# A streaming encoder step on one core: the output projection by token tile, a split router, and a first expert selected without the table

## The chip, the cores and the metric

The kernel runs on one core of one Trainium2 chip. Its time is device time in microseconds. Three runs of the kernel before gave a median of 1534.97 us (1534.58 to 1539.33). Engines are called as in the profile: PE (matmuls), PEld (its weight loads), DVE (vector), ACT (scalar, with activation functions), POOL (GpSimd), SP (the engine that issues nearly all transfers). A "q" behind a name, as in SPq, is that engine's sequencer.

## What is computed

The reference is one inference step of a one-layer streaming encoder, in float32, for 256 tokens of a prompt and 64 tokens of a running stream, all 1024 wide:

```python
mix = jax.nn.sigmoid(ga) * y_att + jax.nn.sigmoid(gb) * y_conv
xp = layer_norm(DN_ALPHA * xp + mix @ w_out[l] + b_out[l], ln1_g[l], ln1_b[l])
ff = moe(xp.reshape(B * S, D_MODEL), w_router[l], b_router[l], w_gate[l], ...)
xp = layer_norm(DN_ALPHA * xp + ff, ln2_g[l], ln2_b[l])
```

`y_att` is chunked band attention, `y_conv` a depthwise convolution with its own norm; both come from one input projection. The stream's 64 tokens go the same way with caches. `moe` is a router over 32 experts: logits from `x @ w_router + b_router`, the 4 largest per token, a softmax over these 4, and for each chosen expert a clamped SwiGLU, `h = gt * sigmoid(1.702 * gt) * (up + 1)`, `h @ w_down + b_down`, summed with the softmax weights. Every expert has three matrices of 1024x1024, 4 MB each: 12.6 MB an expert, 403 MB for all.

## The kernel before

The 320 tokens are three tiles: 128, 128 and 64 rows (`TT`, numbered 0, 1, 2). SBUF holds six weight buffers of 4 MB, `WG`, `WU` and `WD`, each twice, for experts of even and of odd place. In the dense part the same memory holds the activations and a ring of two halves (`ring[0]`, `ring[1]`, 512 columns each) through which the dense weights pass; `WG[1]` is the ring's own memory, `WD[1]` holds `xtok` and `x1T`. The program of each engine is written out by hand, engine by engine, and semaphores set the order; nothing is planned by a tool. In a `wait_ge` the engine's sequencer stops, and all that follows it on that engine waits too.

Around the change the order is this. SP asks for the two halves of `w_out` when the attention's output product has used the ring's halves (line 275, `ao_mm` 4 and 8). PE multiplies half by half: for each half `s`, for each token tile, 8 matmuls of 512 columns into one PSUM bank (line 1132). DVE adds each result to `xtok` (L755), takes statistics (L758), and behind the second half normalises a tile (L761 to L775); ACT supplies the square root (L548). The result is `xs`, kept with channels regrouped. PE transposes tiles 0 and 1 (L1147), ACT copies them out chunk by chunk (L557), PE computes their logits (L1154), then the same for tile 2 with DVE's copy (L794). DVE then does the router for all three tiles at once (L799 to L823): bias, the 8 largest, their indices, one-hot terms, softmax, the mask `chosen`.

From the mask PE counts each token's rank within its expert (L1180), DVE makes `rank`, sorts the experts (a key comparison; places alternate large and small experts, experts 0 and 1 stand first) and writes three tables: `tbl` (the first block of each expert), `nblk`, `order` (L845 to L855, then `tables_done`). A block is up to 32 tokens of one expert. POOL compares ranks with slot numbers to make the selector `sel` (L428 to L437) and copies one-hot columns, `hot` (L441, L442). PE gathers the block's tokens with `sel` (L1214) and turns them (L951).

The loop runs over 16 pairs of experts, and inside over their blocks, 58 in all here. For each pair PE's sequencer loads three table entries into registers:

```python
starts = [pe.value_load(tbl[0:1, bass.ds(q * 2 + k, 1)], min_val=0, max_val=200) for k in range(3)]
```

A block is: gate product (L1231, 64 passes of 32-column weights in four column strips), the previous block's combine (L1254), up product (L1231), gather for the next block, transposes, down product (L1296). SP reloads each half of a weight buffer when the last block of its expert has used it (L235). ACT fills `yacc`, the sum's start, with the scaled `xs` ahead of the loop (L585, L590), and DVE adds each block's result (L867).

## Time and profile before

| what | value |
|---|---|
| median of three runs | 1534.97 us |
| the profiled execution's own time | 1536.92 us |
| its span | 1535.2 us |
| PE busy | 1413.4 us, 92% |
| DVE, ACT, POOL busy | 569.7, 283.5, 116.5 us |
| HBM read | 454.09 MB |
| mean granted clock of PE | 0.965 |

Busy time alone says little here: PE is busy for nine tenths of the span, and the transfers run near their rate for long stretches too, but not in the same stretches throughout. In the profile's 40 slices (38.4 us each) the transfers stand still at about 620 to 650 us, and from 960 to 1490 no slice leaves them below nine tenths. A granted clock of 1.0 is 2.4 GHz, 0.5 is 1.2 GHz; a window between the two had part of each.

### The profile page before, as it was taken

Reading aid. Unit: us, or ns where it says so; the run is one execution under the profiler, and the core shown is the slowest. Engines: PE = TensorE matmul, PEld = TensorE weight load, DVE = VectorE, ACT = ScalarE, POOL = GpSimd, SP = SyncE. Lnnn points to the kernel's source line nnn. Section 1 sums busy time; section 2 is a strip of 40 time slices with the busy share of each in tenths; the row PEclk is TensorE's granted clock in tenths of the full one; section 3 lists DMA queues with packets and bytes.
Section 4 is the critical chain, followed back from the end, with each engine's and each line's share of the span. In section 5 each row is a group of like instructions: output and inputs, shape, how many; then the busy total and the mean of one; then the engine's idle time right before and its main releaser. Section 6 shows DMA issues by size and latency. Waiting matters only on the chain.

```text
span 1535.2 us, 41624 instructions
## 1 busy us (share of the span) xinstructions
PE 1413.4 (92%) x17082; PEld 796.0 (52%) x17083; DVE 569.7 (37%) x1080; ACT 283.5 (18%) x600; POOL 116.5 (8%) x327
## 2 busy tenths in 40 slices
PE   7999999888996899999999999999998998879994
PEld 4777674466644445555545445454454454335542
DVE  1069962233216233332333333333232332213325
ACT  0111211233011312112112112111111111111112
POOL 3500000000000110000010001000100010000100
PEclk9999999899997899999999999999999999999997
DMA  7343332510676797079799797999999999999990
GB/s 230 112 149 123 110 109 75 199 56 1 250 307 263 322 426 305 0 331 427 294 429 423 319 427 301 403 426 425 426 429 424 426 427 426 425 428 428 423 412 34
DMA packets 62981, 458.63 MB, mean 299 GB/s; under 512 B 4325, under 2 KB 6997, under 8 KB 30158
## 3 DMA queue, kind: packets, MB, share of 16 engines
q1 hardware_dynamic: 62698, 457.98, 72.6%
q10 hardware_dynamic: 259, 0.33, 0.1%
q8 instruction: 15, 0.25, 0.1%
q14 instruction: 9, 0.07, 0.0%
HBM read 454.09 MB, written 4.73 MB: 299 GB/s over the span
## 4 chain that ended last, share of the span: by engine, by line
PE 79%; DMA 11%; DVE 4%; issue 2%; ACT 2%; SPq 2%; ACTq 0%; POOLq 0%; POOL 0%; DVEq 0%
PE PS L1231 23%; PE PS L978 14%; PE PS L1296 12%; DMA SB<-in_w_down_dram 10%; PE PS L1254 6%; PE PS L1214 5%; PE PS L951 4%; PE PS L1132 3%; PE PS L1020 3%; PE PS L1111 2%; SPq L235 2%; ACT SB L515 1%; PE PS L1237 1%; PE PS L1241 1%; DMA SB<-in_state_conv_dram 1%
## 5 line engine op out<-in xcount | busy, mean ns | idle before, releaser
L1231 PE MATMUL PS<-SB 128*32 128x256 f32 x7424 | 438.5, 389 | 53.1 <-issue 32.5
L1231 PEld LDWEIGHTS PS<-SB 128*32 128x32 f32 x7424 | 239.5, 112 | 234.7 <-issue 74.2
L867 DVE SCALAR_TENSOR_TENSOR SB<-PS,SB 128x1024 f32<-128x1024 f32 x177 | 194.9, 1101 | 82.1 <-PE PS L1254 82.1
L1296 PE MATMUL PS<-SB 128*32 128x256 f32 x3712 | 213.4, 381 | 4.5 <-DMA SB<-in_w_down_dram 4.5
L978 PE MATMUL PS<-SB 128*128 128x320 f32 x768 | 209.8, 437 | 0.0
L978 PEld LDWEIGHTS PS<-SB 128*128 128x128 f32 x768 | 147.3, 192 | 61.7 <-issue 1.9
L878 DVE TENSOR_SCALAR PS<-PS 128x256 f32<-128x256 f32 x58 | 25.1, 432 | 410.3 <-PE PS L1241 410.3
L1296 PEld LDWEIGHTS PS<-SB 128*32 128x32 f32 x3712 | 114.1, 110 | 85.5 <-issue 9.8
L1254 PE MATMUL PS<-SB 32*128 32x256 f32 (+1 forms) x1416 | 124.0, 419 | 4.0 <-DVE SB L867 3.4
L670 DVE SCALAR_TENSOR_TENSOR SB<-SB 128x350 f32<-128x350 f32 x240 | 118.6, 575 | 0.0
L951 PE MATMUL PS<-SB 128*128 128x128 f32 (+6 forms) x406 | 85.2, 313 | 26.4 <-DVE SB L729 14.2
L1214 PE MATMUL PS<-SB 128*32 128x256 f32 (+1 forms) x1416 | 97.9, 390 | 7.3 <-POOL SB L437 7.3
L598 ACT COPY SB<-PS 128x256 f32<-128x256 f32 x58 | 21.6, 372 | 393.3 <-PE PS L951 393.3
L951 PEld LDWEIGHTS PS<-SB 128*128 128x128 f32 (+6 forms) x406 | 49.4, 164 | 86.3 <-issue 38.7
L885 DVE TENSOR_SCALAR PS<-PS 128x256 f32<-128x256 f32 x58 | 25.1, 432 | 144.8 <-PE PS L1241 144.8
L596 ACT ACT_TABLE_LOAD x58 | 74.4, 1283 | 1.0
L441 POOL CAST SB<-SB 128x1 bf16 x58 | 10.8, 186 | 802.2 <-PE PS L1287 802.2
L1214 PEld LDWEIGHTS PS<-SB 128*32 128x32 f32 (+1 forms) x1416 | 34.0, 108 | 61.8 <-issue 51.8
L1254 PEld LDWEIGHTS PS<-SB 32*128 32x128 f32 (+1 forms) x1416 | 49.3, 166 | 27.0 <-DVE SB L867 4.2
L428 POOL TENSOR_TENSOR SB<-SB 128x96 f32<-128x96 f32 x58 | 20.4, 352 | 526.8 <-issue 523.8
L596 ACT ACTIVATE SB<-PS 128x256 f32<-128x256 f32 x58 | 22.2, 383 | 201.8 <-DVE PS L878 201.8
L604 ACT COPY SB<-PS 128x256 f32<-128x256 f32 x58 | 21.6, 372 | 193.9 <-PE PS L1296 193.9
(203 smaller groups left out, 974.4 us busy)
## 6 DMA issues: line engine op xcount, KB each, us to landing
SB<-in_w_gate_dram SPq DMA_DIRECT2D x64, 2048.0 KB, 25.2
SB<-in_w_up_dram SPq DMA_DIRECT2D x64, 2048.0 KB, 30.4
SB<-in_w_down_dram SPq DMA_DIRECT2D x64, 2048.0 KB, 32.5
SB<-in_w_in_dram SPq DMA_DIRECT2D x14, 2048.0 KB, 8.0
SB<-in_w_pw_dram SPq DMA_DIRECT2D x2, 2048.0 KB, 11.0
SB<-in_w_att_o_dram SPq DMA_DIRECT2D x2, 2048.0 KB, 7.9
SB<-in_w_out_dram SPq DMA_DIRECT2D x2, 2048.0 KB, 8.8
SB<-rev_bias SPq DMA_DIRECT2D x1, 2048.0 KB, 7.8
```

Of the source, the lines that this page charges most:

```text
L235: eng.dma_start(buf[:, 4 * h:4 * h + 4, :], src[:, step * h:step * h + step, :]).then_inc(sem(f"{name}_{h}"), 16)
L596: act.activation(tin, PS[:, 0, 0:256], ACT.Sigmoid, scale=SW_ALPHA).then_inc(sem("sig"), 1)
L670: dve.scalar_tensor_tensor(yc[:, c, :], uext[:, c, bass.ds(k, CONVN)], dwT[:, c, bass.ds(k, 1)], yc[:, c, :], ALU.mult, ALU.add).then_inc( ...
L867: dve.scalar_tensor_tensor(y, ps, gcol[:, tt:tt + 1], y, ALU.mult, ALU.add).then_inc(sem("yadd"), 1)
L951: return pe.transpose(out, in_, ident[0:k, 0:k])
L978: ins = pe.matmul(PS[:, t, 0:T], ring[s][:, c, P * t:P * t + P], xT[:, c, :], start=(c == 0), stop=(c == KC - 1))
L1020: ins = pe.matmul(PS[0:r, bank, :], xT[:, c, t0:t0 + r], ring[s][:, c, :], start=(c == 0), stop=(c == KC - 1))
L1132: ins = pe.matmul(PS[0:r, 3 * s + tt, :], mixT[:, c, t0:t0 + r], ring[s][:, c, :], start=(c == 0), stop=(c == KC - 1))
L1214: ins = pe.matmul(PS[32 * q:32 * q + 32, 2, 0:256], sel[r, tt, :], x_part(tt, q // 2)[:, k], start=(tt == 0), stop=(tt == 2))
L1231: ins = pe.matmul(PS[32 * q:32 * q + 32, bank, 0:256], xg[:, c % 2, c // 2, :], buf[:, c, 256 * q:256 * q + 256], start=(c == 0), stop=False)
L1254: ins = pe.matmul(out, scat[r, TT[tt][0]:sum(TT[tt])], ysb[r, :], start=True, stop=True)
L1296: ins = pe.matmul(PS[32 * n:32 * n + 32, 2, 256:512], hT[:, ck % 2, ck // 2, :], WD[par][:, ck, 256 * n:256 * n + 256], start=(ck == 0), s ...
```

## The change

- **Output projection.** For each token tile, both halves: PE waits for both halves of `w_out` first, then multiplies tile 0, tile 1, transposes tile 0, multiplies tile 2. Tile 2's halves go to partitions 0 to 63 and 64 to 127 of one bank. ACT copies the second half of tile 2's `xtok` to the upper partitions beforehand.
- **Norm and router.** DVE normalises tile by tile. ACT copies each transposed tile in one operation. Tiles 0 and 1 go through the router together, tile 2 alone; the sort's constants and those of the tables are set between the two. The order of experts is sent to PE's queue ahead of the ranks' transposes.
- **First selector.** POOL makes `sel0` for expert 0 right from `rank`, and PE gathers with it before the tables are there. POOL's loop is as before, with its own wait on `sel_ready`; what it makes for block 0 is not used.
- **Tables.** A fourth table `tbl3` packs three block numbers into one integer; PE loads one entry a pair and unpacks it in registers. The wait on `hot_ready` moves from the block's start to the middle of the gate product.
- **The sum `yacc`.** Its start is computed on DVE instead of ACT.

```diff
-            sp.wait_ge(sem("out_mm"), 6)
+            sp.wait_ge(sem("out_mm"), 3)
             load_halves(sp, WG[1], wg_v[1], "wg1")
...
-            sp.wait_ge(sem("logit_mm"), 1)
+            sp.wait_ge(sem("logit_mm"), 2)
             load_halves(sp, WD[1], wd_v[1], "wd1")
...
-            for name in ("gsig", "h_ready", "y_sb", "hT_ready", "bc_mm", "gath_mm"):
+            for name in ("gsig", "h_ready", "y_sb", "hT_ready", "bc_mm", "gath_mm", "sel_ready"):
...
+            pool.wait_ge(sem("rank_ready"), 1)
+            link(pool.tensor_tensor(sel0, rank[:, :, 0:1].broadcast_to([P, 3, SLOTS]),
+                                    iota.rearrange("p (a s) -> p a s", a=1).broadcast_to([P, 3, SLOTS]), ALU.subtract))
+            pool.tensor_scalar(sel0, sel0, 0.0, None, ALU.is_equal).then_inc(sem("sel0_ready"), 1)
...
                     pool.wait_ge(sem("gath_mm"), i + 1)
+                    pool.wait_ge(sem("sel_ready"), i + 1)
...
+            def turned_x1(tt):
+
+                act.wait_ge(sem("x1T_mm"), tt + 1)
+                act.copy(x1T[:, :, P * tt:P * tt + P], PS[:, 2 * tt:2 * tt + 2, :].rearrange("p b (c n) -> p (b c) n", c=4))\
+                   .then_inc(sem("x1T_a"), 1)
+
+            act.wait_ge(sem("xr_ready"), 3)
+            act.copy(xtok[64:128, 2, 512:D], xtok[0:64, 2, 512:D]).then_inc(sem("xr2_ready"), 1)
             std1(0)
+            act.wait_ge(sem("v_out"), 32)
+            turned_x1(0)
             std1(1)
+            turned_x1(1)
             std1(2)
 
-            act.wait_ge(sem("v_out"), 32)
-            for c in range(KC):
...
+                act.wait_ge(sem("top_ready"), 1 + tt // 2)
...
-            act.wait_ge(sem("tables_done"), 1)
...
-            for tt in range(3):
...
-                        act.activation(dst, src, ACT.Copy, scale=ALPHA).then_inc(sem("y_init"), 1)
...
+            act.wait_ge(sem("tables_done"), 1)
...
-            for s in range(2):
-                for tt, (_, r) in enumerate(TT):
-                    dve.wait_ge(sem("out_mm"), 3 * s + tt + 1)
...
+            def norm1(tt):
+
+                r = TT[tt][1]
+                v = xtok[0:r, tt, :]
+                dve.wait_ge(sem("out_mm"), tt + 1)
+                if tt < 2:
+                    w = v.rearrange("p (s n) -> p s n", s=2)
+                    dve.tensor_tensor(w, w, PS[:, 2 * tt:2 * tt + 2, :], ALU.add).then_inc(sem("x1_pre"), 1)
+                else:
+                    for s in range(2):
+                        c, k = slice(512 * s, 512 * s + 512), slice(64 * s, 64 * s + 64)
+                        ins = dve.tensor_tensor(xtok[0:r, 2, c], xtok[k, 2, c], PS[k, 4, :], ALU.add)
+                    ins.then_inc(sem("x1_pre"), 1)
+                dve.wait_ge(sem("x1_pre"), tt + 1)
+                for s in range(2):
+                    ins = dve.bn_stats(stats[0:r, tt, 6 * s:6 * s + 6], xtok[0:r, tt, 512 * s:512 * s + 512])
+                link(ins)
...
+            def largest(tiles, bank):
+
+                n = tiles.stop - tiles.start
+                link(dve.tensor_tensor(lg[:, tiles, :], PS[:, bank, 0:n * E].rearrange("p (t e) -> p t e", t=n),
...
+                dve.tensor_scalar(ntop[:, tiles], top8[:, tiles, 0], -1.0, None, ALU.mult).then_inc(sem("top_ready"), 1)
+
+            def shares(tiles):
+
+                n = tiles.stop - tiles.start
+                for tt in range(tiles.start, tiles.stop):
+                    ins = dve.max_index(idx8[:, tt, :], top8[:, tt, :], lg[:, tt, :])
...
+            dve.wait_ge(sem("logit_mm"), 1)
+            largest(slice(0, 2), 5)
+            dve.wait_ge(sem("v_out"), 32)
+            dve.wait_ge(sem("x1T_mm"), 3)
+            for half in range(2):
+                ins = dve.tensor_copy(x1T[:, 4 * half:4 * half + 4, NP_:T], PS[:, 4 + 3 * half, 0:256].rearrange("p (c n) -> p c n", c=4))
+            ins.then_inc(sem("x1T_d"), 1)
+            shares(slice(0, 2))
+
             link(dve.tensor_copy(tie, iota[0:E, 0:E]))
...
+            link(dve.memset(one_r, 1.0))
+            link(dve.memset(starts, 0.0))
+
+            dve.wait_ge(sem("logit_mm"), 2)
+            largest(slice(2, 3), 6)
+            shares(slice(2, 3))
...
             dve.wait_ge(sem("order_mm"), 1)
-            link(dve.tensor_copy(order, PS[0:1, 2, E:2 * E]))
-            link(dve.tensor_copy(cnt, PS[0:1, 2, 0:E]))
...
             link(dve.tensor_scalar(nb, nb, 1.0, None, ALU.max))
-            link(dve.memset(one_r, 1.0))
-            link(dve.tensor_tensor_scan(cum, one_r, nb, 0.0, ALU.mult, ALU.add))
-            link(dve.memset(tbl[:, 0:1], 0))
-            link(dve.tensor_copy(nblk, nb))
-            dve.tensor_copy(tbl[:, 1:E + 1], cum).then_inc(sem("tables_done"), 1)
+            link(dve.tensor_tensor_scan(starts[:, 1:E + 1], one_r, nb, 0.0, ALU.mult, ALU.add))
+            dve.tensor_copy(nblk, nb)
+            dve.tensor_copy(tbl, starts)
+            link(dve.scalar_tensor_tensor(three, starts[:, 1:E:2], 256.0, starts[:, 0:E:2], ALU.mult, ALU.add))
+            link(dve.scalar_tensor_tensor(three, starts[:, 2:E + 2:2], 65536.0, three, ALU.mult, ALU.add))
+            dve.tensor_copy(tbl3, three).then_inc(sem("tables_done"), 1)
+            dve.wait_ge(sem("tables_done"), 1)
+
+
+            for tt in range(2):
...
-            dve.wait_ge(sem("y_init"), 8)
...
-            for s in range(2):
-                pe.wait_ge(sem(f"ring{s}"), 16 * 10)
-                for tt, (t0, r) in enumerate(TT):
-                    if s == 1 and tt == 1:
-                        pe.wait_ge(sem("ktok_ready"), 6)
-                    for c in range(KC):
-                        ins = pe.matmul(PS[0:r, 3 * s + tt, :], mixT[:, c, t0:t0 + r], ring[s][:, c, :],
-                                        start=(c == 0), stop=(c == KC - 1))
-                    ins.then_inc(sem("out_mm"), 1)
-
...
+            def project(tt):
+
+                t0, r = TT[tt]
                 for c in range(KC):
-                    for tt in tiles:
-                        t0, r = TT[tt]
-                        src = x1_chunk(tt, c)
-                        o = 64 * (c // 4) if tt == 2 else 0
-                        ins = pe.transpose(PS[:, c, t0:t0 + r], src, ident[o:o + r, o:o + r])
-                    ins.then_inc(sem("x1T_mm"), 1)
+                    for s in range(2):
+                        if tt < 2:
+                            out = PS[:, 2 * tt + s, :]
+                        else:
+                            out = PS[64 * s:64 * s + 64, 4, :]
+                        ins = pe.matmul(out, mixT[:, c, t0:t0 + r], ring[s][:, c, :], start=(c == 0), stop=(c == KC - 1))
+                ins.then_inc(sem("out_mm"), 1)
...
+            def turn_x1(tt):
+
+                r = TT[tt][1]
+                pe.wait_ge(sem("x1_ready"), tt + 1)
...
-            pe.wait_ge(sem("x1_pre"), 6)
-            pe.wait_ge(sem("x1_ready"), 2)
-            transposed([0, 1])
-            pe.wait_ge(sem("x1T_a"), KC)
+            for s in range(2):
+                pe.wait_ge(sem(f"ring{s}"), 16 * 10)
+            project(0)
+            project(1)
+            turn_x1(0)
+            pe.wait_ge(sem("ktok_ready"), 6)
+            project(2)
             pe.wait_ge(sem("wr_in"), 32)
-            for tt in range(2):
-                logits(tt)
-            pe.wait_ge(sem("x1_ready"), 3)
-            transposed([2])
+            pe.wait_ge(sem("x1T_a"), 1)
+            logits(0)
+            turn_x1(1)
+            pe.wait_ge(sem("x1T_a"), 2)
+            logits(1).then_inc(sem("logit_mm"), 1)
+            turn_x1(2)
             pe.wait_ge(sem("x1T_d"), 1)
             logits(2).then_inc(sem("logit_mm"), 1)
...
+            for tt in range(2):
+                ranked(PS[:, 7, E * tt:E * tt + E], tt)
+            pe.wait_ge(sem("chosen_ready"), 2)
+            ranked(PS[:, 7, 2 * E:3 * E], 2)
...
+            pe.wait_ge(sem("at_place_ready"), 1)
+            for k in range(2):
+                ins = pe.matmul(PS[0:1, 6, E * k:E * k + E], cols[:, 1 + k:2 + k], at_place, start=True, stop=True)
+            ins.then_inc(sem("order_mm"), 1)
+
             pe.wait_ge(sem("rank_ready"), 1)
             for tt, (t0, r) in enumerate(TT):
                 ins = tr(PS[0:E, 5, t0:t0 + r], rank[0:r, tt, :])
             ins.then_inc(sem("rankT_mm"), 1)
...
-            def gather(need, free):
-
...
+            def gather(sel):
...
                         pe.wait_ge(sem(f"{loaded}_{c // 4}"), count)
+                    if c == 4 and hot_count is not None:
+                        pe.wait_ge(sem("hot_ready"), hot_count)
                     for q in range(Q):
...
+            pe.wait_ge(sem("sel0_ready"), 1)
+            gather(sel0)
+            turn_x(1)
...
-            gather(1, None)
-            turn_x(1)
             with pe.Fori(0, E // 2) as q:
-                starts = [pe.value_load(tbl[0:1, bass.ds(q * 2 + k, 1)], min_val=0, max_val=200) for k in range(3)]
+                three = pe.value_load(tbl3[0:1, bass.ds(q, 1)], min_val=0, max_val=200 * 65793)
+                starts = [three & 255, (three >> 8) & 255, three >> 16]
                 for par in range(2):
                     with pe.Fori(starts[par], starts[par + 1]) as i:
-                        pe.wait_ge(sem("hot_ready"), i * 2 + 2)
...
+                        gate_or_up(0, WG[par], f"wg{par}", q * 16 + 16, 0, "gate_half", "gate_done", i * 2 + 2)
...
-                        gather(i + 2, i + 1)
+                        pe.wait_ge(sem("sel_ready"), i + 3)
+                        pe.wait_ge(sem("tin_x"), i + 1)
+                        gather(sel)
```

## Rows read from the trace of the kernel before

**Rows 1.** Waits in the expert loop, 509 to 1513: total, times, longest.
```profile
PE PS L1231 <- issue: 32.5, 16, 2.6
```

**Rows 2.** Source view of L1264, 540 to 550: count, min/median/max ns, first and last start.
```profile
L1264 PEldq FUSED_REGOPS  x5: 51/151/156, 543.1 to 544.7; - x5
...
L1264 PEldq TENSOR_LOAD <-SB x3: 298/300/307, 542.8 to 544.4; - x3
```

**Rows 3.** Windows: length, busy time of five engines, clock, DMA share, GB/s.
```profile
946.00:962.00 16.00, 16.00 (x270) 8.46 (x266) 5.69 (x10) 3.06 (x6) 1.46 (x5) 1.00 0.22 78
...
962.00:1490.00 528.00, 484.99 (x7706) 251.05 (x7706) 168.18 (x296) 89.03 (x175) 42.07 (x145) 0.98 1.01 426
```

**Rows 4.** Source view of L235 around 543.7: one issue, its landing.
```profile
L235 SPq DMA_DIRECT2D SB<-in_w_down_dram x1: 384/384/384, 543.7 to 543.7; - x1
...
DMA to landing us min/median/max: 32.0/32.0/32.0
```

**Rows 5.** Source view of L235 around 790.3: one issue, its landing.
```profile
L235 SPq DMA_DIRECT2D SB<-in_w_down_dram x1: 383/383/383, 790.3 to 790.3; - x1
...
DMA to landing us min/median/max: 31.2/31.2/31.2
```

**Rows 6.** Timeline of PE at three down products: start, duration, what, idle before.
```profile
574.07 2.80 PE L1296 MATMUL PS<-SB 128*32 128x256 f32 x48
...
820.63 2.58 PE L1296 MATMUL PS<-SB 128*32 128x256 f32 x44
...
1376.26 1.93 PE L1296 MATMUL PS<-SB 128*32 128x256 f32 x32 [0.33 <-DMA SB<-in_w_down_dram]
```

**Rows 7.** Source view of L275, 425 to 445: the second half of w_out.
```profile
L275 SPq DMA_DIRECT2D SB<-in_w_out_dram x1: 379/379/379, 429.5 to 429.5; - x1
...
DMA to landing us min/median/max: 10.0/10.0/10.0
```

**Rows 8.** Timeline from the output projection to the first gate product.
```profile
431.94 41.85 PE L1132 MATMUL PS<-SB 128*128 128x512 f32 x96
...
473.82 0.68 DVE L755 TENSOR_TENSOR SB<-SB,PS 64x512 f32<-64x512 f32 x1 [0.66 <-PE PS L1132]
...
480.33 0.17 DVE L781 COPY SB<-SB 32x32 f32<-32x32 f32 x1
...
487.24 0.26 DVE L799 TENSOR_TENSOR SB<-PS,SB 128x96 f32<-128x96 f32 x1 [2.10 <-PE PS L1154]
...
491.12 0.21 DVE L823 TENSOR_SCALAR SB<-SB 128x96 bf16<-128x96 f32 x1
...
493.72 0.82 PE L951 MATMUL PS<-SB 128*32 128x128 f32 x3
...
494.92 0.18 DVE L845 CAST SB<-PS 1x32 int32<-1x32 f32 x1
...
497.29 0.17 DVE L855 CAST SB<-SB 1x32 int32<-1x32 f32 x1
...
502.20 2.94 PE L1214 MATMUL PS<-SB 128*32 128x256 f32 x24 [7.31 <-POOL SB L437]
...
505.69 0.69 PE L951 MATMUL PS<-SB 128*128 128x128 f32 x2 [0.55 <-ACT SB L570]
...
508.97 5.97 PE L1231 MATMUL PS<-SB 128*32 128x256 f32 x64 [2.59 <-issue]
```

**Rows 9.** Timeline of PE behind a wait in attention.
```profile
296.65 2.54 PE L951 MATMUL PS<-SB 128*128 128x128 f32 x10 [4.26 <-DVE SB L729]
```

**Rows 10.** Windows behind that wait and behind the first gate product.
```profile
300.00:310.00 10.00, 10.00 (x49) 7.82 (x49) 3.12 (x7) 3.28 (x15) 0.00 (x0) 0.72 0.00 1
...
512.00:516.00 4.00, 4.00 (x60) 1.82 (x54) 0.00 (x0) 2.55 (x3) 0.00 (x0) 0.79 0.58 180
```

**Rows 11.** Source view of L235, 473 to 474: first half of expert 1's w_gate.
```profile
DMA to landing us min/median/max: 7.3/7.3/7.3
```

**Rows 12.** Source view of L235, 487.2 to 487.6: expert 1's w_down, both halves.
```profile
DMA to landing us min/median/max: 14.8/17.1/19.3
```

More of the change, by code:

```diff
@@ L201, in encoder_step @@
         nb = view(R0 + 784, E, rows=1)
-        cum = view(R0 + 816, E, rows=1)
-        one_r = view(R0 + 848, E, rows=1)
-        above_n = view(R0 + 880, E, MAXB, rows=1)
+        sel0 = view(R0 + 2208, 3, SLOTS)
+        one_r = view(R0 + 816, E, rows=1)
+        starts = view(R0 + 848, E + 2, rows=1)
+        three = view(R0 + 1432, E // 2, rows=1)
+        above_n = view(R0 + 882, E, MAXB, rows=1)
         tri = view16(R0 + 2048, BF16, P)
@@ L445, in _ @@
             pool.wait_ge(sem("gath_mm"), total + 1)
+            pool.wait_ge(sem("sel_ready"), total + 1)
             pool.tensor_tensor(sel, sel, sel, ALU.subtract).then_inc(sem("sel_ready"), 1)
@@ L578, in _ @@
             turned()
-            for tt in range(3):
-                for half in range(2):
-                    if tt < 2:
-                        dst = yacc[:, D * tt:D * tt + D].rearrange("p (q c) -> p q c", c=KC)[:, :, 4 * half:4 * half + 4]
-                        src = x_part(tt, half).rearrange("p (c q) -> p q c", c=4)
-                        act.activation(dst, src, ACT.Copy, scale=ALPHA).then_inc(sem("y_init"), 1)
-            for half in range(2):
-                dst = yacc[64 * half:64 * half + 64, 2 * D:2 * D + 512].rearrange("p (q c) -> p q c", c=KC)
-                for k in range(2):
-                    src = x_part(2, k).rearrange("p (c q) -> p q c", c=4)[:, 64 * half:64 * half + 64, :]
-                    act.activation(dst[:, :, 4 * k:4 * k + 4], src, ACT.Copy, scale=ALPHA).then_inc(sem("y_init"), 1)
+            act.wait_ge(sem("tables_done"), 1)
             total = act.value_load(tbl[0:1, E:E + 1], min_val=1, max_val=200)
@@ new lines, in _ @@
+            for tt in range(3):
+                norm1(tt)
+            dve.wait_ge(sem("x1_ready"), 3)
+            dve.wait_ge(sem("wr_in"), 32)
+            def largest(tiles, bank):
+                n = tiles.stop - tiles.start
+                link(dve.tensor_tensor(lg[:, tiles, :], PS[:, bank, 0:n * E].rearrange("p (t e) -> p t e", t=n),
+                                       br_bc.rearrange("p (a e) -> p a e", a=1).broadcast_to([P, n, E]), ALU.add))
+                for tt in range(tiles.start, tiles.stop):
+                    ins = dve.max(top8[:, tt, :], lg[:, tt, :])
+                link(ins)
+                dve.tensor_scalar(ntop[:, tiles], top8[:, tiles, 0], -1.0, None, ALU.mult).then_inc(sem("top_ready"), 1)
@@ L781, in _ @@
+            dve.wait_ge(sem("logit_mm"), 1)
+            largest(slice(0, 2), 5)
+            dve.wait_ge(sem("v_out"), 32)
+            dve.wait_ge(sem("x1T_mm"), 3)
+            for half in range(2):
+                ins = dve.tensor_copy(x1T[:, 4 * half:4 * half + 4, NP_:T], PS[:, 4 + 3 * half, 0:256].rearrange("p (c n) -> p c n", c=4))
+            ins.then_inc(sem("x1T_d"), 1)
+            shares(slice(0, 2))
             link(dve.tensor_copy(tie, iota[0:E, 0:E]))
@@ L1181, in ranked @@
                 return ins
-            for tt in range(3):
-                ranked(PS[:, 1, E * tt:E * tt + E], tt)
+            for tt in range(2):
+                ranked(PS[:, 7, E * tt:E * tt + E], tt)
+            pe.wait_ge(sem("chosen_ready"), 2)
+            ranked(PS[:, 7, 2 * E:3 * E], 2)
             for s, (_, r) in enumerate(TT):
-                ins = pe.matmul(PS[:, 1, 3 * E:4 * E], ones16[0:r], chosen[0:r, s, :], start=(s == 0), stop=(s == 2))
+                ins = pe.matmul(PS[:, 7, 3 * E:4 * E], ones16[0:r], chosen[0:r, s, :], start=(s == 0), stop=(s == 2))
             ins.then_inc(sem("rank_mm"), 1)
@@ L1192, in _ @@
             ins.then_inc(sem("gT_mm"), 1)
+            pe.wait_ge(sem("at_place_ready"), 1)
+            for k in range(2):
+                ins = pe.matmul(PS[0:1, 6, E * k:E * k + E], cols[:, 1 + k:2 + k], at_place, start=True, stop=True)
+            ins.then_inc(sem("order_mm"), 1)
             pe.wait_ge(sem("rank_ready"), 1)
@@ L1197, in _ @@
             ins.then_inc(sem("rankT_mm"), 1)
-            pe.wait_ge(sem("at_place_ready"), 1)
-            for k in range(2):
-                ins = pe.matmul(PS[0:1, 2, E * k:E * k + E], cols[:, 1 + k:2 + k], at_place, start=True, stop=True)
-            ins.then_inc(sem("order_mm"), 1)
-            def gather(need, free):
-                pe.wait_ge(sem("sel_ready"), need)
-                if free is not None:
-                    pe.wait_ge(sem("tin_x"), free)
+            def gather(sel):
                 for tt in range(3):
@@ L1223, in turn_x, with gate_or_up @@
                 ins.then_inc(sem("trx_mm"), 1)
-            def gate_or_up(bank, buf, loaded, count, which, half, done):
+            def gate_or_up(bank, buf, loaded, count, which, half, done, hot_count=None):
                 for c in range(KC):
```

119 lines of the change are left out of this document (56 added, 63 removed).

## Prediction, made before the changed kernel was run

> **What bounds the kernel now.** I read the page's slices first, then the waits, the loop's windows and last a timeline of the stage that is rewritten. The run has three stretches. Up to 509 us it is the dense part, where matmuls follow each other with waits between. From 509 to 1512 it is the loop over 58 expert blocks. Two things alternate there. PE works without a pause in most blocks: its idle time of its own is 16 gaps of about 2 us, one per pair of experts [rows 1]. The weight stream is the other: from 962 to 1490 it moves 426 GB/s at a DMA share of 1.01, while just before, from 946 to 962, it stood at 0.22 because PE had not yet freed a buffer [rows 3]. So up to 960 PE sets when the stream restarts. From there the stream sets the pace, until PE's last wait on a weight ends at 1376.26 [rows 6]; after it PE alone sets the end. There are four such halts of the stream (600 to 659, 750 to 760, 851 to 858, 950 to 960; the row is of the last). A shift of the first block therefore runs through to the end, but a gain made inside the loop survives only where no landing stands behind it.
>
> Two landings decide that. The last half of w_down of expert 3 is issued at 543.7 and lands 32.0 later, at 575.7 [rows 4]; PE begins that product at 574.07 and needs the half 1.8 us in (64 passes at 58 ns, from 48 in 2.80), at 575.9 [rows 6]. There is no room (0.2). For expert 9 it is 790.3 + 31.2 = 821.5 against 820.63 + 1.8 = 822.4, room 0.9 [rows 5, 6]. Experts 6 and 12, the other two at the end of such a run of transfers, have 2.9 and 4.4 by the same reckoning.
>
> **The output projection.** Before: 48 matmuls (96 passes) in 41.85 us from 431.94, 6.98 per tile and half [rows 8]. It could start because only the first half of w_out was asked for. The second half is issued at 429.5 and takes 10.0, so it lands at 439.5 [rows 7]. The new order asks for both halves ahead of the first matmul, and all of PE is queued behind that wait: PE starts at 439.5, 7.6 later than now. Tiles 0 and 1 cost 4 x 6.98 = 27.9. The 64-row tile's two halves run in two column strips at once: one pass of 512 columns takes 0.436 (41.85 / 96), which is 0.218 for 256 columns, and the loop's four strips take 0.058 a pass, 3.8 times less; so strips overlap nearly fully and I take 7.0 instead of 14.0. Ends: 7.0, and 14.0 if they don't overlap. Tile 0's transposes come between: 8 of them, 1.0 (an estimate from three small ones in 0.82 at the lower clock).
>
> The wait also costs clock. After an idle of 4.26 the granted clock fell to 1.2 GHz and was there for 56% of the next ten us, although PE ran [rows 9, 10]. At the first gate product it came back 4.7 us after the start (0.79 over 512 to 516) [rows 8, 10]. The wait here is longer, so I take the fall as sure, 4.7 us at half rate, loss 2.3; ends 0 and 4.5 (nine us low, as in attention). The projection then ends at T = 439.5 + 27.9 + 1.0 + 7.0 + 2.3 = 477.7, against 473.8 before. So this part alone makes things 3.9 later.
>
> **What T decides.** Expert 1's w_gate goes into the ring's place and is issued at T. Its first half lands 7.3 after issue, at 481.1 [rows 11], and the last half of its w_down at 487.6 + 19.3 = 506.9 [rows 12]: 33.1 from issue to the sixth half. The issue of w_down moves with the router from 487.2 to 490.6, while the stream has work to 499: nothing. Before, the stream then stood still until 512.8. If the first reload is issued early enough, it now follows without a pause, 12 more halves of 2.097 MB at 426 GB/s = 4.92 each to expert 3's last one: T + 33.1 + 59.0 = 569.8 against 575.7. The stream gains 5.9, or 483.6 - T in general.
>
> **Norm, router, tables.** Tile 2's norm is last: before, 6.5 us from the projection's end to 480.33 [rows 8]. It now has a second addition and a second statistics pass behind that end (0.7 each, by the 0.68 row), 7.9 in all: 485.6. Tile 1's norm ends at 477.4 and is not in the way, but ACT is: the square root of tile 2 is queued behind the copy of tile 1's transposes, and these stand on PE behind tile 2's projection and tile 0's logits (2.4 and 1.0, copy 1.1, so 482.2), where DVE would want it at 480.8. That wait costs 1.4: x1 is ready at 487.0 (480.3 before). Transposes 0.7, copies 0.8, logits 1.9 end at 490.6. DVE meanwhile does the router of two tiles, and now the constants too, which stood under a wait before: 0.9 + 0.8 + 2.5 + 1.1 to 492.3. Then tile 2's router alone: three tiles took 487.24 to 491.33 = 4.1, most of it fixed cost, one tile 2.6 as an estimate: 494.9, which is 3.5 later than before.
>
> Behind it a lot goes. The tables come 6.1 behind the mask (497.46), now 0.2 less: 500.8. The order is on DVE 2.5 ahead of them, so PE is through with it at 498.2 and turns the ranks in 0.8: 499.0. The selector for expert 0 no longer waits for the tables and POOL's three loads; its two POOL operations are done by then. Gather 2.94, copy 0.5: the transposes start at 502.4. From their start to the gate it was 3.28 with three table loads; with one it is 2.1: gate at g = 504.5 against 508.97, 4.5 earlier. The reload is issued 3.9 behind g and lands 7.3 after: 515.7, where the stream allows 515.7 (481.1 + 3.9 + 25.8 + 4.9). So the stream's 5.9 just holds; each microsecond that g is later takes one away.
>
> **The yacc initialisation** moves from ACT to DVE, which idled until the first clamp: eight operations, at most 6.2 us from 500.8, three loads 2.4: 509.4; the first clamp is due at 511. Nothing; if DVE is late by 2, PE waits for less than that. **The hot wait** moves from the gate's start to its middle: POOL writes it for later blocks long before; nothing, at most 0.1 a block either way. **POOL's own wait** on the selector: nothing.
>
> **One table load instead of three.** Loads start 0.8 apart (542.8 to 544.4) [rows 2]. Two fewer is 1.6; unpacking adds four register operations, which take 0.05 to 0.15 each: 0.4. That leaves 1.2 a pair. Ends: -0.2 (the unpacking costs what the loads did) and 1.7. Where it counts: at the second pair it is lost to expert 3's landing (no room). Pairs 3 and 4 keep 2.4 (room 2.9), pair 5 keeps 0.9 of 1.2 (expert 9), pairs 6 and 7 keep 2.4 (room 4.4): 5.7 by 960. Then seven pairs are lost to the stream. The last two (gaps before 1396 and 1462) keep 2.4. Sum 8.1.
>
> **The sum.** 5.9 + 8.1 = 14.0; nothing changes behind 1512. The profiled execution took 1536.92 for a span of 1535.2; the median shown is 1534.97, so 1536.92 - 14.0 = 1522.9 would be that execution's twin, and from the median it is 1521.0, which I take.
>
> **A page of the skill weighed.** The Trainium skill, "TensorE: Matmul & The Clock Gate", section "Measured speedup vs the span model", has three column strips at 2.38 times, not 3. By that rate two strips give 1.6, tile 2 costs 8.8 and the time is 1522.8. The trace has 3.8 of 4 and I go by it; the page's rate has 5 of the forecast's 59 chances in 100.
>
> **Rivals.**
> (A) The strips run one after another: T = 484.7, the stream gains -1.1, total 7.0: 1528.0. Against it stands the 0.058. 8%.
> (B) The pair savings don't arrive, 5.9 alone remains: 1529.1. For it: assertion and unpacking also take register time [rows 2]; against it: the loads' spacing. 12%.
> (C) The clock doesn't fall at the wait: T = 475.4, the stream gains 8.2 and g moves along, total 16.3: 1518.7. 8%.
> (D) The chain through ACT and DVE is 4.5 longer than summed: the first gate comes no earlier than now and 8.1 remains: 1526.9. For it: every step of it is linked to the one before; against it: most steps are rows of the old chain. 8%.
> (E) Slower. The clock falls at the wait and does not come back during the projection: 69.8 instead of 34.9, T = 511.3 with the transposes, the stream loses 27.7, total 19.6 later: 1554.6. It decides from 33 us at the low rate, where T passes 491.7. For it: nine low us behind the attention wait [rows 9, 10]; against it: these are the densest matmuls of the kernel. 5%.
> The Trainium skill, same page, section "Loop structure matters more than you think", speaks for (E): matmuls that stand behind a wait for a transfer run cold. The trace agrees that they start so.
>
> **Numbers.** Forecast 1521.0, 59%, its own range 1517 to 1525 (clock 0 to 4.5, load 1.0 to 1.7, g). The range 1515 to 1529.5 takes in A to D. 0.3%, 4.6 us, is about what a measurement of this kernel can tell from no change. Faster: the forecast and A to D but for the thin end of B and D, 0.91; within 0.3%: 0.04; slower: E, 0.05.
>
> **What would show it.** Right: PE idle for 7.6 before the projection with a clock below 1 behind it; 32 passes of 128x64 weights in 7.0; the first gate near 504.5; gaps between pairs at 0.8; a stream with no halt between 480 and 600; PE waiting over a microsecond for expert 3's w_down. Wrong: a first gate after 506, gaps near 2.0, or the projection ending past 480.

## The result, and the profile after

The changed kernel took 1516.34 us (median of 4, 1514.17 to 1518.34), the kernel before beside it 1535.43 (1534.58 to 1539.33): a ratio of 0.987, 95% interval 0.985 to 0.989. That is 19.1 us less, where 14.0 was forecast. The span of the profiled execution went from 1535.2 to 1512.5, 22.7 less. A repeat of the changed kernel, below called the repeat, gave 1516.42 (4 runs) with a profiled span of 1515.6. One run of a version below, the one that keeps PE busy while it waits, was a slow one (1617.63, at a granted clock of 0.871) and is left out of that version's median.

The rewritten stage, timeline of PE and DVE in the kernel after:

```profile
436.93 29.19 PE L1180 MATMUL PS<-SB 128*128 128x512 f32 x64 [6.85 <-DMA SB<-in_w_out_dram]
466.93 7.09 PE L1180 MATMUL PS<-SB 128*64 128x512 f32 x32
473.94 1.97 PE L1198 MATMUL PS<-SB 128*128 128x32 f32 x16
478.09 0.15 DVE L775 RECIPROCAL SB<-SB 64x1 f32<-64x1 f32 x1 [1.10 <-ACT SB L557]
490.58 0.18 DVE L829 TENSOR_SCALAR SB<-SB 128x32 bf16<-128x32 f32 x1
494.88 2.94 PE L1262 MATMUL PS<-SB 128*32 128x256 f32 x24
496.78 0.17 DVE L886 CAST SB<-SB 1x16 int32<-1x16 f32 x1
500.25 5.35 PE L1281 MATMUL PS<-SB 128*32 128x256 f32 x64 [1.50 <-issue]
```

PE waits 6.85 for w_out's second half, the two strips of tile 2 take 7.09, ACT holds DVE for 1.10, the gather starts ahead of the last table copy, and the first gate product comes at 500.25. Against [rows 8] everything from there on is sooner.

Waits of PE in the loop (total, times, longest), then windows (columns as in [rows 3]) and SP's issues:

```profile
PE PS L1281 <- DMA SB<-in_w_up_dram: 15.0, 9, 2.2
PE PS L1349 <- DMA SB<-in_w_down_dram: 9.0, 8, 1.9
PE PS L1281 <- DMA SB<-in_w_gate_dram: 8.9, 5, 3.0
PE PS L1281 <- issue: 8.2, 15, 1.5
```

```profile
430.00:440.00 10.00, 3.15 (x5) 1.52 (x5) 0.00 (x0) 2.83 (x4) 0.00 (x0) 0.66 1.02 382
...
946.00:962.00 16.00, 16.00 (x270) 8.45 (x266) 5.69 (x11) 3.06 (x6) 1.46 (x5) 1.00 1.01 433
```

```profile
410.27 17.61 SPq L278 DMA_DIRECT2D SB<-in_w_out_dram  x2
474.05 0.81 SPq L238 DMA_DIRECT2D SB<-in_w_gate_dram  x2
503.05 3.51 SPq L238 DMA_DIRECT2D SB<-in_w_gate_dram  x2
```

In the wait and behind it the clock is low: 0.66 in the mean from 430 to 440. The 32.5 us that PE lost between pairs [rows 1] are 8.2, and a window in which the stream stood nearly still [rows 3] is now full of it, at 433 GB/s. Three more timeline rows of PE: a gap between pairs, and the waits for the last half of w_down of expert 3 and of expert 27, which is the last weight that PE waits for (1376.26 in [rows 6]):

```profile
534.63 3.66 PE L1281 MATMUL PS<-SB 128*32 128x256 f32 x64 [0.48 <-issue]
566.42 1.93 PE L1349 MATMUL PS<-SB 128*32 128x256 f32 x32 [1.32 <-DMA SB<-in_w_down_dram]
1358.21 1.93 PE L1349 MATMUL PS<-SB 128*32 128x256 f32 x32 [1.85 <-DMA SB<-in_w_down_dram]
```

These points cut the run in four. w_out is asked for at 412.28 in the profile of before:

| stretch | before | after | repeat | gain | forecast |
|---|---|---|---|---|---|
| start to the issue of w_out (code unchanged) | 412.3 | 410.3 | 411.2 | 2.0, 1.1 | 0 |
| to expert 3's last half | 163.4 | 156.1 | 158.3 | 7.3, 5.1 | 5.9 |
| to the last weight that is waited for | 800.6 | 791.8 | 791.8 | 8.8 | 5.7 |
| to the end | 158.9 | 154.3 | 154.3 | 4.6 | 2.4 |

The first line is no gain: over the profiles shown here, of fourteen executions, the unchanged dense part reaches that issue between 407.6 and 414.2. Without it the change is worth 20.7 and 18.5 in the two traces, 19.1 in the medians. The split between the other lines is good to about 2 us only: a second trace of the kernel before (below) has 161.6, 798.8 and 160.6 in them, where the first has 163.4, 800.6 and 158.9.

### The profile page after: what moved, and what is told of

Its sections match the earlier page's. It is cut to its first block, busy times and chain, and to the rows that moved or that the text cites. A ratio compares the mean times of both kernels' runs of the same rounds, so it can differ in the third digit from the quotient of the medians.

```text
span 1512.5 us, 41579 instructions
## 1 busy us (share of the span) xinstructions
PE 1405.4 (93%) x17082; PEld 790.8 (52%) x17083; DVE 575.4 (38%) x1100; ACT 277.7 (18%) x587; POOL 117.3 (8%) x329
## 4 chain that ended last, share of the span: by engine, by line
PE 72%; DMA 18%; DVE 4%; SPq 2%; ACT 2%; issue 1%; ACTq 0%; DVEq 0%
PE PS L1281 20%; DMA SB<-in_w_down_dram 17%; PE PS L1022 14%; PE PS L1349 11%; PE PS L1304 5%; PE PS L1262 5%; PE PS L995 3%; PE PS L1064 3%; PE PS L1155 2%; PE PS L1180 2%; SPq L238 2%; ACT SB L524 1%; PE PS L1287 1%; PE PS L1291 1%; DMA SB<-in_state_conv_dram 1%
## 5 line engine op out<-in xcount | busy, mean ns | idle before, releaser
L449 POOL CAST SB<-SB 128x1 bf16 x58 | 10.8, 186 | 778.7 <-PE PS L1340 778.7
L472 ACT ACTIVATE SB<-PS,SB 128x320 f32 x40 | 21.1, 528 | 130.5 <-PE PS L1022 130.4
```

## Experiments

The theory after the result, called the stream theory, in its last form: up to expert 27 the end is set by when weight halves land, and that hangs on two issues alone, expert 1's w_gate (behind the projection) and the first reload (in the first gate product). Behind expert 27 it is PE's work. The rivals are that each microsecond of PE's own work counts (work theory), and, for each part, that it did nothing. In the expectations it is an earlier form, in which the second issue has some room. All times are medians of 3 to 8 runs; the kernel before gave 1535.6, 1536.4 and 1535.9 in the three groups of runs.

**Three table loads instead of one.**

```diff
-three = pe.value_load(tbl3[0:1, bass.ds(q, 1)], ...)
-starts = [three & 255, (three >> 8) & 255, three >> 16]
+starts = [pe.value_load(tbl[0:1, bass.ds(q * 2 + k, 1)], ...) for k in range(3)]
```

> PE again loads three table entries a pair instead of one packed entry; all else as changed. Stream theory (a gain in the loop counts only where no landing of weights stands behind it): gaps of 2.0 instead of 0.48, 1.5 each, kept in the pairs 3 to 7 up to the room of the landings and in the last two; 8 to 10 us, and up to 13.4 if the granted clock falls again at some of the 2 us gaps: 1525 to 1530. Rival 1 (every gap counts): 15 x 1.5 = 23, 1539. Rival 2 (the loop is bound by transfers, gaps are worth nothing): 1516 to 1518.

Measured: 1528.35, ratio 0.995 (0.993 to 0.996), 11.9 more than the changed kernel, within the stream theory's 1525 to 1530 and far from both rivals. PE in its trace:

```profile
505.39 5.12 PE L1281 MATMUL PS<-SB 128*32 128x256 f32 x64 [3.01 <-issue]
672.00 3.66 PE L1281 MATMUL PS<-SB 128*32 128x256 f32 x64 [1.88 <-issue]
1370.31 1.93 PE L1348 MATMUL PS<-SB 128*32 128x256 f32 x32 [1.87 <-DMA SB<-in_w_down_dram]
```

A gap is 1.88 in place of 0.48, so the packed table saves 1.40 a pair, not 1.2. From expert 3's half (572.18) to 1370.31 it is 798.1 against 791.8 and from there to the end 157.0 against 154.3: the load is worth 6.3 and 2.7 there. The first reload, which is now the later of the two issues by 1.8 (last table), makes 10.8 of the 11.9.

**The packed table in the kernel before, alone.**

```diff
+dve.scalar_tensor_tensor(three, starts[:, 1:E:2], 256.0, starts[:, 0:E:2], ...)
+dve.scalar_tensor_tensor(three, starts[:, 2:E + 2:2], 65536.0, three, ...)
+dve.tensor_copy(tbl3, three).then_inc(sem("tables_done"), 1)
...
-starts = [pe.value_load(...) for k in range(3)]
+three = pe.value_load(tbl3[0:1, bass.ds(q, 1)], ...)
+starts = [three & 255, (three >> 8) & 255, three >> 16]
```

> The kernel before with the packed table alone: one table load in place of three at each pair, everything else of it as before. Stream theory: the first gate comes 1.4 earlier, and as the stream stands still then, expert 3's weights land 1.4 earlier; pairs 3 to 7 keep what the landings of experts 6, 9 and 12 leave room for (2.9, 0.8 and 2.9, with 1.7 more if the clock's fall at the gap before 874 goes too); after the last landing two gaps of 1.45 each, and 1.7 if the fall before 1462 goes. Sum 11.0 without the clock's falls, 14.4 with them: 1521.2 to 1524.6, and gaps of 0.5 us in place of 2.0. Work theory (all 16 gaps count): 23 less, 1512. The prediction's own price, 1.2 a pair and 8.1 in the loop: 1527.5. It also tells whether the falls of the clock at three of the gaps go with the gaps' length or with another part of the change.

Measured: 1521.37, ratio 0.991 (0.989 to 0.992). This one edit alone gives 15.0, where the whole change gives 19.1. Its gaps are 0.56 to 0.63, and no gap in its trace has a fallen clock behind it.

**The hot wait in the middle, in the kernel before, alone; and back at the start, in the changed kernel.**

```diff
 def gate_or_up(...):
     if c % 4 == 0: pe.wait_ge(sem(f"{loaded}_{c // 4}"), count)
+    if c == 4 and hot_count is not None: pe.wait_ge(sem("hot_ready"), hot_count)
 ...
-pe.wait_ge(sem("hot_ready"), i * 2 + 2)
```

> The kernel before with the hot wait in the middle of the gate's product, as in the changed kernel, and nothing else. The gaps between pairs should be 1.88 in place of 1.98 to 2.03. If the clock's falls at three of the gaps (5.35 in place of 3.66 for the product behind) hang on this tenth of a microsecond, they go, as in the changed kernel with three loads, and the time is 0.3 plus up to 3.4 less: 1532 to 1533. If they are a matter of chance or of place, they stay in part and the time is 1535 to 1536.

Measured: 1530.89, ratio 0.996 (0.995 to 0.998): 5.0 less for a tenth of a microsecond a gap, more than the 1532 to 1533 that were expected if the falls hang on it. The kernel before was traced once more:

> The kernel before once more, for a second trace of it. If the three falls of the clock at the gaps belong to the kernel, the products behind the gaps at about 874, 1058 and 1462 take 5.35 again; if they are chance, they stand elsewhere or there are more or fewer. Time as before: 1534 to 1539.

Measured: 1536.27. Gate products behind a gap in the first trace of before (one), in the second (four), then in that with the wait moved:

```profile
874.28 5.35 PE L1231 MATMUL PS<-SB 128*32 128x256 f32 x64 [2.00 <-issue]
```

```profile
872.59 3.66 PE L1231 MATMUL PS<-SB 128*32 128x256 f32 x64 [1.98 <-issue]
988.97 5.35 PE L1231 MATMUL PS<-SB 128*32 128x256 f32 x64 [1.99 <-issue]
1392.54 5.35 PE L1231 MATMUL PS<-SB 128*32 128x256 f32 x64 [2.01 <-issue]
1460.41 5.35 PE L1231 MATMUL PS<-SB 128*32 128x256 f32 x64 [1.98 <-issue]
```

```profile
872.84 3.66 PE L1233 MATMUL PS<-SB 128*32 128x256 f32 x64 [1.88 <-issue]
1458.77 3.66 PE L1233 MATMUL PS<-SB 128*32 128x256 f32 x64 [1.87 <-issue]
```

Each trace lists 14 such products between pairs. In the first of before 3 of 14 took 5.35 in place of 3.66 (at 874, 1058, 1462), in the second 4 (989, 1231, 1392, 1460); in the second, the 20 us from 1460 have a mean clock of 0.91, those from 860 have 1.00. With gaps of 1.87 to 1.93, here and with three loads above, none of 28 did, nor did any with the packed table (3.66 to 3.81). A fifteenth gap stands before half a product, 32 passes, and is not in these counts; behind it they took 1.93, but 2.41 in the second trace of before. So the clock's falls are chance in place, were seen, of the gaps between pairs, behind those of 1.97 to 2.03 alone, and cost 1.7 each where PE's work counts. The stretch behind expert 27 shows it in each trace: 157.0 without a fall, 158.9 with one, 160.6 with two. All this is for gaps in else dense work: among close waits for weights the clock is low around shorter ones too (in the kernel after 0.50 from 1338 to 1342, behind waits of 2.95 and 1.88), which costs nothing where the stream sets the pace.

The traces with and without each of the two edits, from expert 3's last half to the end:

| | hot wait at the start | hot wait in the middle |
|---|---|---|
| three loads | 959.5, 959.4 (before, twice) | 955.2, 955.1 (hot wait moved; three loads) |
| one packed load | 946.6, 946.2 (before with the packed table; the run that follows) | 946.1, 946.1 (changed, repeat) |

With three loads the hot wait is worth 4.3 here, with one load 0.1 to 0.5: either edit takes the falls away, and there is nothing left for the other to take. Only the sum is steady: against the two traces of before the moved wait gives 2.4 and 0.6 up to expert 27, and 1.9 and 3.6 behind it.

The other way round, in the changed kernel:

> The changed kernel with the hot wait back at the start of each block. For the first block POOL writes it 1.3 us behind the gate's start (504.18 against 502.87), so that gate comes 1.3 later; that lies within the room of the first reload. The gaps between pairs get 0.10 to 0.12 longer (0.48 to 0.58), and two of them count at the end. Stream theory: 0.2 to 0.5 more, 1516.6 to 1516.9. Work theory: 1.3 and 16 times 0.11, 3.1 more, 1519.5.

Measured: 1517.19 (ratio 0.988, 0.986 to 0.990), 0.8 more than the changed kernel and not to be told from it. Its trace shows the first gate waiting 3.30 for POOL's copy, the first reload at 503.72 and expert 3's half at 566.69; by the last table its first reload is the later issue by 1.9, so "within the room" was wrong.

**The strips one behind the other.**

```diff
 order = [(c, s) for c in range(KC) for s in range(2)]
+if tt == 2: order = [(c, s) for s in range(2) for c in range(KC)]
```

> Tile 2's two column strips are multiplied one after the other (8 matmuls of one strip, then 8 of the other) instead of in turn. Stream theory: the projection ends 7 us later (14 instead of 7.1) and the end 7 us later: 1523. Rival 1 (the strips overlap nothing anyway, or the time is hidden): 1516. Rival 2 (the first gate binds, and its chain absorbs part): 1518 to 1521.

Measured: 1521.28, ratio 0.990 (0.989 to 0.992), 4.9 more. Tile 2 in its trace:

```profile
472.35 12.29 PE L1182 MATMUL PS<-SB 128*64 128x512 f32 x32
484.57 0.63 PE L1200 MATMUL PS<-SB 128*128 128x32 f32 x4
```

12.29 against 7.09: what the order by turns saves is 5.2, not 7. Even strip by strip the 32 passes take less than the 14.0 of no overlap, apparently because the last passes of the one strip run beside the first of the other (the 2 us from 477 hold 10 passes, those before them 6). So the expected 1523 had the wrong price; at the right one the 4.9 is one for one with the projection's end. The second rival, that the first gate binds, was put at 1518 to 1521 and is not excluded by the time; in this trace the two issues stand 0.3 apart (last table). Side by side, the two strips' 32 passes (7.09) cost what 16 cost on full columns (6.98 in the forecast's rows).

**Tile 0 by halves**, so that PE starts before the second half of w_out lands.

```diff
+if tt == 0: order = [(c, s) for s in range(2) for c in range(KC)]
+if tt == 0 and c == 0: pe.wait_ge(sem(f"ring{s}"), 16 * 10)
...
-for s in range(2): pe.wait_ge(sem(f"ring{s}"), 16 * 10)
```

> Tile 0 is multiplied half by half again, so that PE waits for the second half of w_out only after 6.9 us of work; tiles 1 and 2 as changed. Stream theory: PE's idle of 6.85 before the projection and the 1.3 of low clock behind it go, the projection ends 8 us earlier and so does everything up to the end: about 1508. Rival (the projection's end is not what the stream waits for, a later link binds): less than 3 us, 1513 to 1516.

Measured: 1508.33, ratio 0.982 (0.981 to 0.984), 8.1 less than the changed kernel.

```profile
431.03 7.03 PE L1184 MATMUL PS<-SB 128*128 128x512 f32 x16
438.72 20.87 PE L1184 MATMUL PS<-SB 128*128 128x512 f32 x48 [0.66 <-DMA SB<-in_w_out_dram]
467.41 1.97 PE L1202 MATMUL PS<-SB 128*128 128x32 f32 x16
```

**PE kept busy in that wait**, without starting sooner.

```diff
+pe.wait_ge(sem("ktok_ready"), 6)
+for n in range(8): pe.matmul(PS[:, 7, :], mixT[:, n, 0:P], ring[0][:, n, :], ...)
+pe.wait_ge(sem("ring1"), 16 * 10)
```

> The changed kernel with eight extra matmuls of 128x512 on w_out's first half (16 passes, 7.0 us, into a bank that nothing reads) while PE waits for the second half. If the idle time is what lets the clock fall, it stays high: the first 64 passes of the projection take 27.9 in place of 29.2 to 29.7, and the time is 1.3 to 1.8 less, 1514.6 to 1515.1. If the fall comes from something else (the smaller products ahead of it), 1516.4. If the extra matmuls outlast the transfer, up to 1 us is given back and it is 1516 too, but the trace then shows passes at full clock.

```profile
428.37 7.10 PE L1205 MATMUL PS<-SB 128*128 128x512 f32 x16 [0.99 <-ACT SB L552]
435.31 27.67 PE L1180 MATMUL PS<-SB 128*128 128x512 f32 x64
```

The mechanism is shown: 27.67 for the 64 passes, against 29.19 in the kernel after and 29.65 in the repeat. The time, 1512.16 (3 runs; ratio 0.985, 0.983 to 0.987), is 4.3 less where 1.3 to 1.8 were due. In this trace w_out was asked for at 407.56, the earliest of all. From there to the end it takes 1102.0, where the changed kernel takes 1102.2 and the repeat 1104.4. So 0.2 to 2.4 are gained behind that issue, as due, and the rest is the start, in code that was not changed. Why it was early was not settled.

**Expert 1's w_gate asked for later.** Nothing else is touched.

```diff
 sp.wait_ge(sem("out_mm"), 3)
+sp.wait_ge(sem("logit_mm"), 1)
 load_halves(sp, WG[1], wg_v[1], "wg1")
```

> The changed kernel, with one wait more on SP alone: expert 1's w_gate is asked for when the logits of tiles 0 and 1 are through (484.1 in the trace of the changed kernel's repeat) in place of the projection's end (476.6). PE, DVE and ACT do what they did, and expert 1's last half still lands some 20 us before its use. Stream theory: every later landing moves by the 7.5, up to the stream's last one at 1361, and the time with it: 1523.9. Work theory (a transfer with 20 us of room costs nothing): 1516.4. Prediction's view, 1 for 1 as long as no halt stands behind: 1523.9 too, so this run tells only between the first two.

Measured: 1523.94, ratio 0.992 (0.991 to 0.993). PE's own part up to the gather is as in the repeat, and the last half of expert 1's w_down (issued 489.4, landing 27.9 later) is there 17 us before PE begins that product at 534.2. Still 7.5 us are lost, as the stream theory expected; the work theory had 1516.4:

```profile
483.84 0.82 SPq L238 DMA_DIRECT2D SB<-in_w_gate_dram  x2
506.72 3.59 SPq L238 DMA_DIRECT2D SB<-in_w_gate_dram  x2
```

```profile
476.69 1.97 PE L1199 MATMUL PS<-SB 128*128 128x32 f32 x16
576.22 1.93 PE L1350 MATMUL PS<-SB 128*32 128x256 f32 x32 [0.28 <-DMA SB<-in_w_down_dram]
1368.06 1.93 PE L1350 MATMUL PS<-SB 128*32 128x256 f32 x32 [0.28 <-DMA SB<-in_w_down_dram]
```

**The selector behind the tables again.**

```diff
 pool.wait_ge(sem("rank_ready"), 1)
+pool.wait_ge(sem("tables_done"), 1)
 link(pool.tensor_tensor(sel0, ...
```

> The changed kernel, but POOL builds the first expert's selector only after the wait for the tables, as before. In the trace of the changed kernel POOL would so begin 3.1 us later and the first gate product come 3.1 us later (506.0 in place of 502.9). Stream theory (what counts is when the weight halves land): the first reload, issued at 505.0, would be issued at 508.1 and land 7.3 to 10 later, at 515.4 or after; it landed at 515.3 in any case. So nothing is lost on the stream, and PE has 3.3 us of waits for weights up to expert 3's w_down that take the delay in: 1516.4 to 1518, the upper end if the clock falls in the longer wait. Work theory (every microsecond of the first gate counts): 1519.5. Prediction's statement that there is no slack and each microsecond of a later first gate costs one: 1519.5 as well.

Measured: 1520.52, ratio 0.989 (0.987 to 0.991), 4.1 more. The stream theory as it then stood expected 1516.4 to 1518 and missed; my room of 3.3 was wrong. The work theory's 1519.5, and the prediction's "each microsecond that g is later takes one away", were nearer. The second issue came into the theory after this run: the first reload comes 3.9 later behind the projection than in the repeat, and it is the later issue by 2.8 (table below). The gather begins 4.0 later behind the projection, not 3.1:

```profile
500.84 2.52 DVE L894 TENSOR_SCALAR SB<-SB 128x512 f32<-128x512 f32 x4
500.98 0.75 POOL L422 TENSOR_TENSOR SB<-SB 128x96 f32<-128x96 f32 x1 [441.29 <-DVE SB L887]
501.81 1.07 POOL L424 TENSOR_SCALAR SB<-SB 128x96 f32<-128x96 f32 x1
502.94 2.94 PE L1263 MATMUL PS<-SB 128*32 128x256 f32 x24 [4.13 <-POOL SB L424]
510.30 2.47 SPq L238 DMA_DIRECT2D SB<-in_w_gate_dram  x2
```

POOL's two operations take 0.75 and 1.07 beside the wide ones (128x512) of DVE's yacc initialisation, and in the repeat, with DVE at small work, 0.35 and 0.47:

```profile
494.89 0.35 POOL L421 TENSOR_TENSOR SB<-SB 128x96 f32<-128x96 f32 x1 [435.61 <-DVE SB L858]
495.33 0.47 POOL L423 TENSOR_SCALAR SB<-SB 128x96 f32<-128x96 f32 x1
```

The Trainium skill, "GPSIMD Engine Reference", section "1. Specifications", says that POOL shares its way into SBUF with the vector engine and contends with some of its forms. The slowing above fits that, but no run shows whether these operations are of those forms. Beside the narrower ones (64x256) that follow in the changed kernel, POOL's L436 takes 0.35 as ever.

**The chain to the first gate shortened**, on top of tile 0 by halves: the best version that these results point to.

```diff
 std1(1)
-turned_x1(1)
 std1(2)
+turned_x1(1)
```

(And the constants of the sort move behind `shares(slice(2, 3))` on DVE.)

> The split wait (projection of tile 0 by halves, 1508.3) with two steps taken out of the chain to the first gate: ACT takes tile 2's square root before it copies tile 1's transposes (DVE waited 1.1 for it), and the constants of the order stand behind the router of tile 2 in DVE's queue, where it waits for a bit of PE less (0.85). The first gate comes 1.1 to 2.0 earlier. Stream theory: the landings up to expert 12 hang on the projection's end alone and on the last ones of the ring, which don't move, so nothing is gained: 1508.0 to 1508.6. Work theory: 1506.4 to 1507.2.

Measured: 1507.25, ratio 0.982 (0.981 to 0.984), the same ratio as tile 0 by halves alone. Its first gate comes 24.4 behind the projection's end, where it was 26.2, and this bought nothing that can be measured. The run doesn't tell between the theories either: 1508.0 to 1508.6 and 1506.4 to 1507.2 were expected, and the interval is 2 us to either side. Both versions beat the changed kernel and the one before.

**One rule for all of them.** From the traces: when expert 1's w_gate is asked for (a), when the first reload is (b), and when expert 3's last half is there, by PE's wait or, in the first three lines, by issue and landing. The last columns test it: the later of a + 92.4 and b + 62.9.

| kernel | a | b | expert 3's half | a + 92.4 | b + 62.9 |
|---|---|---|---|---|---|
| before | 473.8 | 512.8 | 575.7 | 566.2 | **575.7** |
| before, second trace | 473.7 | 510.9 | 573.8 | 566.1 | **573.8** |
| before, hot wait moved | 472.6 | 512.0 | 574.7 | 565.0 | **574.9** |
| before, packed table | 472.5 | 508.3 | 571.3 | 564.9 | **571.2** |
| changed, three loads | 477.7 | 509.0 | 572.2 | 570.1 | **571.9** |
| changed | 474.1 | 503.1 | 566.4 | **566.5** | 566.0 |
| changed, repeat | 476.6 | 505.0 | 569.5 | **569.0** | 567.9 |
| PE kept busy | 470.9 | 499.1 | 563.5 | **563.3** | 562.0 |
| tile 0 by halves | 467.5 | 497.4 | 560.2 | 559.9 | **560.3** |
| and the shorter chain | 466.2 | 493.5 | 558.7 | **558.6** | 556.4 |
| strips apart | 484.7 | 513.9 | 577.1 | **577.1** | 576.8 |
| w_gate asked for later | 483.8 | 506.7 | 576.2 | **576.2** | 569.6 |
| hot wait at the start | 472.3 | 503.7 | 566.7 | 564.7 | **566.6** |
| selector behind tables | 478.0 | 510.3 | 573.2 | 570.4 | **573.2** |

It holds within 0.5 us in fourteen traces. The two constants were chosen on these same traces, and no run was forecast with them, so this is a fit and not a test; the forecast's own figure in place of 92.4 was 92.1. In the kernel before the reload was the later by 9.5; the change took that away, and now the two stand within 0.5 to 1.1 of each other.

## Why the prediction held, step by step

- **What bounds the kernel.** Right: the stream from T, then PE behind expert 27. T is not alone, though: the first reload is nearly as late. The asked-for-later w_gate cost 7.5 as computed.
- **The projection.** T was to come 65.4 behind the issue of w_out (477.7 less 412.3). The traces with the projection as changed give 63.4 to 66.1 (473.94 less 410.27 is 63.7, the repeat 65.3). The wait was 6.58 to 8.24 for 7.6; the clock's loss 1.3 in the kernel after, 1.8 in the repeat and 2.4 where w_gate is asked for later, for 2.3; the strips 7.09 for 7.0. Rival A, strips without overlap, would have shown 14.0. The 2.38 for three strips that the prediction weighed, from the Trainium skill, "TensorE: Matmul & The Clock Gate", section "Measured speedup vs the span model", did not show in these two strips: they overlapped fully (7.09 where one takes 6.98).
- **Norm, router, tables.** First gate at T + 26.3 for T + 26.8. ACT's queue cost 1.10 for 1.4. The first reload came 2.8 behind the gate (2.1 in the repeat) for 3.9.
- **What T decides.** Expert 3's half at T + 92.5 for T + 92.1. "The stream's 5.9 just holds" was right to 0.5 us.
- **Yacc and POOL's wait.** Nothing shows, as forecast, though no run takes them out alone. Yacc leaves DVE idle for 4.9 before the first clamp.
- **One table load.** The place was right, the size too small: 1.40 a gap where 1.2 was forecast, since the unpacking is one fused register operation and not four. By the three-loads run it gives 9.0 (6.3 + 2.7) in the loop, for 8.1.
- **The hot wait and the clock behind the gaps.** The step that failed. A gap between pairs was priced at its length alone, 1.2 for the loads and "nothing, at most 0.1 a block either way" for the hot wait; the clock behind a gap had no term in the sum, although the products of 5.35 were there to be read in the trace of before. With the tenth a gap they make 4.3 to 4.4 of the time behind expert 3's half. Either edit removes them: the hot wait alone gives 4.3 there and 5.0 in the medians, the packed table alone 12.9 (959.5 less 946.6) where its length accounts for 9.0. In the changed kernel, with one load, moving the hot wait is worth nothing that can be measured, so that line taken by itself came out as written.

So 14.0 became 19.1: 0.9 more from the load's length and 4.4 from the clock make 19.3. The forecast stood 4.7 above the result for that reason, just outside its own range of 1517 to 1525 and inside the wide one. By the time alone C (1518.7) was nearer than the forecast, but its mechanism was not the one: the 29.19 shows that the clock did fall at the wait. B (the pair savings don't arrive) is refuted by the packed table alone, 15.0; D by the first gate; E by the clock, which came back about 3 us behind the start of the projection in the kernel after and within 7 in every trace with that wait.

The parts don't add: the packed table alone gives 15.0, and all but the packed table (three loads against the kernel before) 7.3, together 22.3 for 19.1. Both take the same falls of the clock away, by the table above, which is more than the 3.2 of difference.

## What to carry to other kernels

Write the landing of the first buffer that PE will wait for as the later of two or three issues plus constants, and read from the trace which of them is the later and by how much: an edit pays on that one, for just that much. A transfer with 17 us of room before its use still costs one for one when the queue behind it is the bound. And an idle gap has two prices, its own length and the clock behind it; here a tenth of a microsecond decided the second.

## What the runs showed of the hardware

- With PE else dense, gaps of 1.97 to 2.03 us were followed by a product at reduced clock (5.35 in place of 3.66) in 7 of 28 cases, and gaps of 1.87 to 1.93 in none of 28. Why, and whether anything changes sharply between them, is not shown.
- A register load on PE's sequencer takes 0.30 to 0.32 but costs 0.7 to 0.8: two loads less one unpacking saved 1.40, and the starts of three lie 0.8 apart [rows 2]. Unpacking three values from one took one fused register operation of 0.16.
- Two strips of 64 columns, multiplied by turns, cost what one costs (7.09 against 6.98). In the order strip by strip they still overlap for part of the way (12.29, not 14).
- POOL's small operations took twice as long beside DVE's 128x512 ones: 0.75 and 1.07 against 0.35 and 0.47. Beside its 64x256 ones a like one did not (0.35).
- The unchanged dense part takes 407.6 to 414.2 up to the issue of w_out. That spread is larger than most of the edits here, so two traces are best compared from that issue on.
